# One level of Strassen's scheme in the up product of an MLP, and a norm by pairs of tiles

## The reference

```python
mix = jnp.concatenate([a, r], axis=-1) @ w_o[i]
x = x + rmsnorm(mix, norm_mix_post[i])
h = rmsnorm(x, norm_mlp_pre[i])
m = jnp.square(jax.nn.relu(h @ w_up[i])) @ w_down[i]     # w_up 1024x4096, w_down 4096x1024
x = x + rmsnorm(m, norm_mlp_post[i])
```

## Time and profile before

| | us |
|---|---|
| median of 3 runs | 1511.26 (1509.25 to 1512.78) |
| the profiled execution, its own time | 1515.07 |
| its span, first to last instruction | 1513.1 |
| PE busy | 1480.3 |
| DVE busy | 646.1 |
| ACT busy | 549.5 |
| POOL busy | 667.4 |

### The profile page before, as it was taken

The page is one execution under the profiler, slowest core; times in us unless marked ns, Lnnn a source line. Parts: engine busy times, 40 slices in busy tenths (PEclk is TensorE's granted clock), DMA queues, the critical chain, the costliest instruction groups (busy, mean ns, idle before and its releaser), DMA issues.

```text
span 1513.1 us, 18913 instructions
## 1 busy us (share of the span) xinstructions
PE 1480.3 (98%) x7192; PEld 1210.0 (80%) x7192; DVE 646.1 (43%) x892; ACT 549.5 (36%) x1036; POOL 667.4 (44%) x539
## 2 busy tenths in 40 slices
PE   6999999999999999999999999999999999999998
PEld 5888888878657778877888888888888888888876
DVE  6135554355676664347404122330413223461465
ACT  5223232234245554435324233332423233343452
POOL 4373535275100003545445455554544445554481
PEclk9999999999999999999999999999999999999999
DMA  5221110012230004322333333333333332333252
GB/s 195 63 63 42 29 36 23 24 36 56 63 84 1 1 1 154 132 84 83 119 95 94 99 97 98 97 98 98 98 98 97 96 97 96 97 118 98 78 166 84
DMA packets 82954, 124.31 MB, mean 82 GB/s; under 512 B 14641, under 2 KB 31025, under 8 KB 82865
## 3 DMA queue, kind: packets, MB, share of 16 engines
q1 hardware_dynamic: 82864, 123.11, 26.9%
HBM read 116.79 MB, written 4.19 MB: 80 GB/s over the span
## 4 chain that ended last, share of the span: by engine, by line
PE 93%; DVE 3%; issue 1%; ACT 1%; POOL 1%; DMA 0%; SPq 0%; DVEq 0%; POOLq 0%; ACTq 0%
PE ps L50 25%; PE ps L52 25%; PE ps L51 25%; PE ps L911 3%; PE ps L1437 3%; PE ps L1455 3%; PE ps L1445 2%; PE ps L1294 1%; PE ps L1004 1%; PE ps L958 1%; PE ps L943 1%; PE ps L955 0%; PE ps L999 0%; PE ps L887 0%; DMA x_tile<-in_x 0%
## 5 line engine op out<-in xcount | busy, mean ns | idle before, releaser
L1229 POOL TENSOR_TENSOR wy_low<-w_raw,wy_high 128x512 fp32r<-128x512 f32 x320 | 442.7, 1384 | 436.9 <-ACT wy_high L1209 436.6
L1209 ACT ACTIVATE wy_high<-w_raw 128x512 fp32r<-128x512 f32 x320 | 202.1, 632 | 560.2 <-PE ps L52 552.5
L50 PE MATMUL ps<-a_high,wy_high 128*128 128x512 f32 x512 | 200.3, 391 | 0.0
L51 PE MATMUL ps<-a_low,wy_high 128*128 128x512 f32 x512 | 199.5, 390 | 0.0
L52 PE MATMUL ps<-a_high,wy_low 128*128 128x512 f32 x512 | 199.5, 390 | 0.0
L50 PE MATMUL ps<-wy_high,hid_high 128*128 128x512 f32 x512 | 199.4, 389 | 0.0
L52 PE MATMUL ps<-wy_high,hid_low 128*128 128x512 f32 x512 | 199.2, 389 | 0.0
L51 PE MATMUL ps<-wy_low,hid_high 128*128 128x512 f32 x512 | 199.2, 389 | 0.0
L362 POOL TENSOR_TENSOR wx_low<-w_raw,wx_high 128x512 fp32r<-128x512 f32 (+1 forms) x64 | 85.0, 1335 | 150.7 <-ACT wx_high L463 150.7
L52 PEld LDWEIGHTS ps<-a_high,wy_low 128*128 128x128 f32 x512 | 96.3, 188 | 20.1
L51 PEld LDWEIGHTS ps<-a_low,wy_high 128*128 128x128 f32 x512 | 96.4, 188 | 19.9
(11 more groups left out here) (196 smaller groups left out, 2494.7 us busy)
## 6 DMA issues: line engine op xcount, KB each, us to landing
w_raw<-in_w_up SPq DMA_DIRECT2D x128, 256.0 KB, 2.7
w_raw<-in_w_down SPq DMA_DIRECT2D x128, 256.0 KB, 2.6
w_raw<-in_w_in SPq DMA_DIRECT2D x62, 256.0 KB, 2.8
w_raw<-in_w_o SPq DMA_DIRECT2D x32, 256.0 KB, 2.6
w_raw<-in_w_ple_gate SPq DMA_DIRECT2D x32, 256.0 KB, 2.6
x_tile<-in_x SPq DMA_DIRECT2D x8, 512.0 KB, 8.2
x_res<-in_x SPq DMA_DIRECT2D x8, 512.0 KB, 5.5
y<-x_res SPq DMA_DIRECT2D x16, 256.0 KB, 2.0
```

The source lines that it names most:

```text
L50: pe.matmul(out, stat_high, mov_high, start=start, stop=False)
L51: pe.matmul(out, stat_high, mov_low, start=False, stop=False)
L1209: act.activation(out, w_raw[:, q % RING, :], ACT.Copy).then_inc(high_made, 1)
L1229: pool.tensor_tensor(low_tile, w_raw[:, q % RING, :], high_tile.bitcast(F32), ALU.subtract).then_inc(low_made, 1)
```

## The change

**The scheme.** The middle 2048 columns of `w_up` (f = 2 to 5) are taken in 8 blocks of 256 columns. A block is a 2 x 2 product: weights b11, b12, b21, b22 (512 rows x 128 columns each) by activations a11 to a22 (512 rows x 512 tokens each). Before, it takes 8 products of 4 x 3 matmuls; now 7, in Winograd's form: four sums of activations S1 to S4 made once, four sums of weights t1 to t4 for each block on POOL, and seven additions for each block on DVE. A block is now the segments `st` (7 weight tiles, 84 matmuls) and twice `dq` (2 rows' tiles of `w_down` by 8 banks, 48 matmuls each). The first pair of column groups of h = 1 uses `d4` segments (4 tiles, 48 matmuls) in place of `dp`; D010 and D011 below are its first two.

**Room.** S1 to S4 and their parts lie where x, a part of `a_high` and `a_low`, and hidden tiles lay. So x (8 x 512 KB) and the part of a (2 x 1 MB) are stored to HBM ahead and loaded back behind the blocks.

**The norm.** Mean and root are formed for two tiles and not four.

```diff
+            ST_BLOCKS, ST_FIRST, ST_COLS = 8, 2 * BANK, 2 * P
+            st_order = ["b11", "t2", "b21", "t3", "t1", "t4", "b22"]
+            st_banks = [0, 1, 0, 2, 3, 4, 3]
...
+            for b in range(ST_BLOCKS):
+                segs += [("st", b, 0, 0), ("dq", b, 0, 0), ("dq", b, 0, 1)]
...
+                        if s == D010 and k == 2:
+                            act.wait_ge(a_kept, 32)
+                            act.wait_ge(done, done_at["bank", U11, 7, 3])
+                            s_high_of(1, s_parts[2])
+                            act.wait_ge(s_split, 4)
+                            act.wait_ge(s_step, 16)
+                            s_high_of(3, s_parts[3])
+                        if (s, k) == (D010 + 2, 3):
+                            act.wait_ge(s_step, 22)
+                            s_high_of(4, s4_raw)
+                        if (s, k) == (D00 + 1, 2):
+                            act.wait_ge(s_step, 10)
+                            s_high_of(2, s_parts[1])
...
-                    for t in range(4):
+                    for t in range(3):
                         add7(o + t)
-                    means7x(h)
+                    means7x(o)
+                    add7(o + 3)
...
+                def strassen(s, b):
+                    dve.wait_ge(done, done_at["prod", s, 1])
+                    dve.wait_ge(u_first, b + 1)
+                    dve.tensor_tensor(u2[:, :], relu[:, 0, :], ps[:, 1, :], ALU.add).then_inc(u2_made, 1)
+                    dve.wait_ge(done, done_at["prod", s, 2])
+                    dve.tensor_tensor(relu[:, 0, :], relu[:, 0, :], ps[:, 0, :], ALU.add).then_inc(st_sum, 1)
+                    dve.wait_ge(done, done_at["prod", s, 3])
+                    dve.wait_ge(u2_made, 2 * b + 1)
+                    dve.tensor_tensor(u3[:, :], u2[:, :], ps[:, 2, :], ALU.add).then_inc(u3_made, 1)
+                    sum_square(4 * b)
+                    sum_low(4 * b)
+                    dve.wait_ge(u3_made, b + 1)
+                    for q, base, k in ((1, u3, 4), (2, u3, 5), (3, u2, 6)):
+                        dve.wait_ge(done, done_at["prod", s, k])
+                        if q == 3:
+                            dve.wait_ge(u2_made, 2 * b + 2)
+                        dve.tensor_tensor(relu[:, q, :], base[:, :], ps[:, st_banks[k], :], ALU.add).then_inc(st_sum, 1)
+                        if q == 1:
+                            dve.tensor_tensor(u2[:, :], u2[:, :], ps[:, st_banks[k], :], ALU.add).then_inc(u2_made, 1)
+                        sum_square(4 * b + q)
+                        sum_low(4 * b + q)
...
+                    elif kind == "dq" and n == 0:
+                        if i == 0:
+                            pe.wait_ge(st_sum, 4 * f + 1)
...
+                        elif i < 5:
+                            pe.wait_ge(st_sum, 4 * f + (4 if i == 3 else 3))
...
+                    elif kind == "dq" and i in (0, 4):
+                        pe.wait_ge(st_hid, 4 * f + (1, 3, 4, 2)[2 * k + i // 4])
```

More of the change, by code:

```diff
@@ L1114, in back_of @@
                         done_at["turn", a, b, part] = count
+                elif kind == "mm" and segs[a][0] == "st":
+                    count += 1
+                    done_at["prod", a, b] = done_at["tile", first[a] + b] = count
                 elif kind == "mm":
@@ L1198, in back_of, with tile_raw, raw_ready @@
                                             "stored"))
[L1199 to L1201 removed]
+            def tile_raw(tile):
+                raw = raw_of(tile)
+                if raw is None:
+                    s, k = tiles_of[tile[1]]
+                    return t_sum[int(st_order[k][1])][:, :]
+                return w_raw[:, raw_at[raw] % RING, :]
+            def raw_ready(engine, raw):
+                q = raw_at[raw]
+                engine.wait_ge(loaded[q % RING], 16 * (q // RING + 1))
+            def high_of(act, tile):
+                raw = raw_of(tile)
+                if raw is not None:
+                    raw_ready(act, raw)
+                else:
+                    s, k = tiles_of[tile[1]]
+                    act.wait_ge(low_made, place["sum", st_order[k], segs[s][1]] + 1)
                 if tile[0] == "res":
@@ L1208, in high_of @@
                         act.wait_ge(done, done_at["tile", tile[1] - PAIRS])
-                act.activation(out, w_raw[:, q % RING, :], ACT.Copy).then_inc(high_made, 1)
+                act.activation(out, tile_raw(tile), ACT.Copy).then_inc(high_made, 1)
             def high(act, n):
@@ L1566, in act_tail @@
                     behind = segs[s - 1][0] if s else None
[L1567 to L1573, removed]
+                    if kind == "st":
+                        strassen(s, f)
+                        continue
+                    for k in range(depth[kind]):
+                        if kind == "dq" and n == k == 0:
+                            sum_relu(4 * f + 3)
+                            sum_high(4 * f + 3)
                         high(act, first[s] + k + AHEAD)
@@ L1706, in hidden_all, with s_chain @@
                 def hidden_all(s):
-                    for q in range(1, 4 if segs[s][0] == "up4" else 8, 2):
+                    for q in range(1, 4, 2):
                         hidden(s, q, hid_first[s] + q)
+                def s_chain(out, parts):
+                    for n in range(1, len(parts)):
+                        for c in range(2):
+                            here = (slice(None), slice(2 * c, 2 * c + 2), slice(None))
+                            sign, part = parts[n]
+                            left = out if n > 1 else parts[0][1]
+                            if n > 1:
+                                dve.wait_ge(s_step, s_steps[0] - 1)
+                            dve.tensor_tensor(out[here], left[here], part[here],
+                                              ALU.add if sign > 0 else ALU.subtract).then_inc(s_step, 1)
+                            s_steps[0] += 1
@@ L1951, in pe_tail @@
                     pe.wait_ge(low_made, place["pair", n] + 1)
+                    if segs[a][0] == "st":
+                        strassen(a, b, wy_high[:, n % PAIRS, :], wy_low[:, n % PAIRS, :]).then_inc(done, 1)
+                        continue
                     for i in range(width):
```

313 lines of the change are left out of this document (258 added, 55 removed).

## The result

The changed kernel takes **1486.41 us** (median of 4 runs, 1485.41 to 1487.03), against 1512.02 (4 runs, 1509.25 to 1514.59) for the kernel before beside it: a ratio of 0.9826, 95% interval 0.9811 to 0.9841. The forecast was 1486 (1480 to 1498), faster. The profiled execution took 1487.03, with a span of 1485.2.

The account below looks back on a forecast made before the run. TensorE bounds the kernel, busy 98% of the span. From the profiled 1515.07: -21.7 - 9.0 + 4.5 + 0.2 + 0.3 = -25.7 gives 1489.4; that execution being 3.8 above the median, the forecast is 1486 us, range 1480 to 1498.

Parts of the forecast that it names:

- Seven products: In the 8 blocks, one product of 12 matmuls fewer each: 96 x 0.2257 = 21.7 us less.
- Norm by pairs: Norm ahead of the MLP: both 2.7 us waits for `h_tile` go, with the clock loss behind them, 9.0 us less.
- Operand sums: New DVE ops forming activation sums S1 to S4, at three places: 0, 4.5 and 0.2 us more.
- The first place: Operand sums from the end of the hidden tiles at 742.9: cost 0, within half a microsecond.
- The second: Operand sums after U11: ACT waits for DVE's lows of S1, PE idle 3.2 us plus 1.3 for clock, 4.5 more.
- The third: S4 before the last down stretch: weight tile ready near 863.4, wanted at 863.2, 0.2 us more.
- Combining on DVE: Each block's DVE chain: last sum ends at T+1.2, bank 3 needs it at T+2.0; cost 0, 0.8 us spare.
- rival 1: Handovers of 0.1 us over ten steps make bank 3 up to 1.5 us late per block: about 1497; chance 0.17.
- Weights, the way through HBM, the room in a bank: Three costs forecast at 0: weight tiles ready in time, x and a reloaded from HBM, 12 matmuls into one bank.
- Rival 2: Copies through HBM starve the weights near the end of the blocks: 1495 us; chance 0.07.
- Rival 3: Six DVE squares and lows per block each meet a POOL instruction; last sum 5.4 us late, 1529 us; chance 0.05.
- Rival 4: Matmuls go but waits only move, needing 23 us of new waits; time within 0.2% (3 us); chance 0.02.

Follow-up runs that it names:

- twice: Changed kernel with the first of the seven products of each block issued twice; 1508.95 us, ratio 0.998.
- split: Changed kernel with ACT's high parts of S3 moved two slots later in its order and those of S4 one slot; 1479.98 us, ratio 0.9796.
- split3: Changed kernel with ACT's high parts of S3 alone moved one slot later, S4 left in place; 1485.04 us, ratio 0.9823.
- extra1: Changed kernel with one more DVE reduction, its result unread, ahead of the last sum of each block; 1488.94 us, ratio 0.9851.
- extra2: Changed kernel with two more DVE reductions, results unread, ahead of the last sum of each block; 1494.72 us, ratio 0.9886.
- extra4: Changed kernel with four more DVE reductions, results unread, ahead of the last sum of each block; 1511.35 us, ratio 0.9998.
- the norm experiment: Two kernels: the changed kernel with the norm by fours again, 1497.08 us; the kernel before with the norm by pairs alone, 1504.58 us.
- norm4: Changed kernel with the norm's mean and root formed for four tiles, as before; 1497.08 us, ratio 0.9903.

## Why the prediction was right, point by point

**Seven products, -21.7.** Right (-21.8 at 0.2267 us). `twice` measures +21.9 for the same 96 matmuls.

**Norm by pairs, -9.0.** Right in mechanism, 0.7 too much: 8.3 by the stretches in all three comparisons. The scaling didn't come just in time but 0.2 us late at both turns, and that costs 0.41 each: from the last matmul before the turn (642.71) to the ninth behind it (646.08) it is 3.37 us, where an undisturbed turn takes 2.96.

**Operand sums.** The first place was forecast at 0 with half a microsecond to spare, and cost 0: ten sums took from 731.50 to 750.59, 19.1 us for the forecast 20.3. The second was forecast at 4.5 (3.2 of wait, 1.3 of clock). It is 3.0 of wait; from 822.18 to 829.78 the PE took 7.60 us for 12 matmuls that are worth 2.72, so 4.9 in all. What comes on top of a wait is 1.9 and not 1.3: the prediction had 1.8 from the earlier trace rows and took a part of it off for the transposes, without a row for that. That it's this place, and for this reason, `split` and `split3` show. The third was forecast at 0.2 and has a wait of 0.36, which by the rule above costs 0.64.

**Combining on DVE, 0 with 0.8 us to spare.** The 0 was right, and the 0.8 was not: 0.44 were left. Counted from the first matmul of the down product (958.52), the last sum ended at 1.55 us, not at 1.2. The 0.35 arise in one stretch. With T for this matmul, as in the prediction, the first low ends at 953.55, which is T-4.97 for the forecast T-4.9, but the second at 956.69, T-1.83 for T-2.2. Between them the square of 954.84 starts 0.77 us behind the sum before it and not 0.6, since it waits for ACT's relu (to 954.81), and then meets a split. From there on the chain took 3.38 us for the forecast 3.4. A handover from one engine to the next took 0.03 to 0.05 us where the trace has it (the sum that ends at 954.14, relu from 954.18; relu to 954.81, square from 954.84), so rival 1's 0.1 over ten steps was too much. The median of 1.40 that the prediction gives for squares beside POOL is that of all 64 squares in the earlier trace rows; it was no term of the sum. One more DVE operation in a block costs 2.4 us (`extra1`).

**Weights, the way through HBM, the room in a bank: 0.** No wait shows in any of these places, and PE is busy throughout.

**The sum.** -21.8 - 8.3 + 4.9 + 0.6 = -24.6, where the prediction had -25.7; its 0.3 for other margins stands against nothing. The stretches give -8.3 - 16.5 = -24.8, the medians -25.6. So the terms were right to about a microsecond, and the errors of 0.7 (norm) and 0.4 (second and third place, each) have the same sign, towards too large a gain, with only the 0.3 against them. That the median of 1486.41 falls within half a microsecond of the forecast is partly luck, since the front alone varies by more. The offset of 3.8 us that I took from the profiled execution of before to the median was real, too: against the profiled execution of after, the front took 3.1 us more in it, at a lower clock.

**The rivals.** Rival 1 (bank 3 late each block) didn't happen, but was 0.44 us away. In `extra1`, `extra2` and `extra4` bank 3 is late by 0.16, 0.76 and 1.96 us and a block takes 0.30, 0.91 and 2.08 more, so 1.5 us late would have cost about 8 x 1.6 = 13 (an estimate), and more where the clock falls. Rival 2: 394 GB/s, no wait. Rival 3: two meetings with POOL and not six; `extra4` shows that it needs 2.4 us of more DVE work in each block to lose the whole gain. Rival 4: the waits of the norm went and didn't move, as both directions of the norm experiment show; new ones came behind U11 alone, for 4.9 + 0.6 us, where this rival wanted 23.

**The best version.** `split`, 1479.98 us: a ratio of 0.9796 to the kernel before. From D00 it is 5.4 us faster than the changed kernel, 1.6 of which is a lower clock that doesn't follow every time. The prediction named the wait that it removes.

## What to carry to other kernels

When an engine that works in order gets an instruction that waits for another engine, count how many of its own later products are needed before that wait ends, and put the instruction behind them; here that was worth 5.4 us for two lines. When a chain over several engines is placed on paper, follow each operation to the slower of its inputs, as the square behind ACT's relu; test the margin that is left by adding one short operation, and look at the period of the blocks and not at the table of waits. Compare two executions by stretches between events that both have, since the unchanged front of this program alone varies by 3 us.

## What the runs showed of the hardware

- A start of a matmul that is up to 0.16 us late is in no table of waits, since the record of the one before (0.39 us) covers it. It cost 0.30 us a time (`extra1`).
- Behind each of the waits for a weight tile or a sum, from U11 to the last block, the second matmul starts 0.34 us after the first and not 0.23: 0.11 us that no row calls a wait.
- Whether a wait of PE is followed by the lower clock isn't settled by its length. The same wait of 3.0 us behind U11 was followed by it in four kernels' executions (the changed one, `norm4`, `extra1` at once, `twice` 1.6 us later) and not in two (`extra2`, `extra4`); of eight waits of 1.79 us four were; of eight of 0.60 us none, and the one of 1.38 us not. The waits of 2.7 us in the norm were, all four of two executions. Where it came behind U11 or in a block it began 0.3 to 1.6 us behind the restart, with the PE at full work between, lasted for about eight matmuls at 0.43 us, and cost 1.60 us. What decides it, these runs leave open.
